# State loads in mid stage, packs from the diagonal down, and the MLP's normed input begun during the output projection

## The reference, cut to what matters

```python
def rmsnorm(x, g):
    y = xf * lax.rsqrt(jnp.mean(xf * xf, axis=-1, keepdims=True) + EPS)
    return y * g
...
for l in range(DEPTH):
    mix = mlstm_layer(...) if l < N_SELF else stick_breaking_attention(q, k_all, v_all, ...)
    h = h + mix @ w_out
    u = rmsnorm(h, norm_mlp[l]) @ w_up[l]
    h = h + jnp.square(jax.nn.relu(u)) @ w_down[l]
# stick-breaking, per head: A[t,s] = beta_ts * prod_{s<j<t}(1 - beta_tj), for s < t strictly
# mLSTM, per sequence: returns h and the final states (c, n, m)
```

## Time and profile before

| | us |
|---|---|
| median of 3 runs | 3212.4 |
| profiled execution, device time | 3211.99 |
| its span | 3210.2 |
| TensorE busy | 2914.1 (91%) |
| VectorE busy | 1363.2 (42%) |
| ScalarE busy | 857.8 (27%) |
| GpSimd busy | 769.2 (24%) |

### The profile page before, as it was taken

How to read it: one execution, slowest core, us unless ns; L and a number is a source line. 1 busy time by engine, 2 the same in 40 slices (tenths; PEclk the granted TensorE clock), 3 DMA queues, 4 the chain that set the end, 5 groups by cost and what they waited for, 6 DMA issues and landing times. The chain is left out here.

```text
span 3210.2 us, 49314 instructions
## 1 busy us (share of the span) xinstructions
PE 2914.1 (91%) x19749; PEld 2646.6 (82%) x19749; DVE 1363.2 (42%) x1993; ACT 857.8 (27%) x1677; POOL 769.2 (24%) x452
## 2 busy tenths in 40 slices
PE   5979698999999999988988889888799999999996
PEld 4968586989999999976666666666598999999995
DVE  4323233353334444344555554554525433334442
ACT  3111212131011111123545455545503111011114
POOL 3211120323322233331211121110032333322230
PEclk8999897999999999998999999999899999999997
DMA  5664413322222222223333333333411111111111
GB/s 154 189 153 138 87 34 15 107 88 84 91 91 91 91 91 91 91 76 100 110 100 105 106 106 109 97 108 86 148 57 40 47 46 40 45 46 46 46 46 60
DMA packets 362481, 277.66 MB, mean 86 GB/s; under 512 B 31394, under 2 KB 353954, under 8 KB 360290
## 3 DMA queue, kind: packets, MB, share of 16 engines
q1 hardware_dynamic: 341002, 258.18, 27.2%
q10 hardware_dynamic: 21336, 17.47, 2.6%
HBM read 251.58 MB, written 91.11 MB: 107 GB/s over the span
## 5 line engine op out<-in xcount | busy, mean ns | idle before, releaser
L162 POOL CAST w_hi<-w_raw 128x1024 fp32r<-128x1024 f32 x194 | 209.0, 1077 | 1725.7 <-PE bank L214 945.3
L212 PE MATMUL bank<-x_hi,w_hi 128*128 128x352 f32 x1872 | 605.2, 323 | 4.2 <-DVE p_q L1743 4.2
L214 PE MATMUL bank<-x_hi,w_lo 128*128 128x352 f32 x1872 | 602.0, 322 | 0.0
L213 PE MATMUL bank<-x_lo,w_hi 128*128 128x352 f32 x1872 | 601.5, 321 | 0.0
L212 PE MATMUL bank<-p_u_hi,w_hi 128*128 128x352 f32 x1536 | 496.5, 323 | 14.6 <-DVE p_u_lo L1947 14.6
L164 POOL TENSOR_TENSOR w_lo<-w_raw,w_hi 128x1024 fp32r<-128x1024 f32 x194 | 494.5, 2549 | 15.5
L213 PE MATMUL bank<-p_u_lo,w_hi 128*128 128x352 f32 x1536 | 495.5, 323 | 0.0
L214 PE MATMUL bank<-p_u_hi,w_lo 128*128 128x352 f32 x1536 | 495.3, 322 | 0.0
L1955 DVE TENSOR_TENSOR h<-bank,h 128x352 f32<-128x352 f32 x384 | 200.0, 524 | 492.4 <-PE bank L214 492.4
L1915 ACT ACTIVATE p_relu<-bank 128x352 f32<-128x352 f32 x192 | 89.3, 465 | 1042.7 <-PE bank L214 1032.9
L212 PEld LDWEIGHTS bank<-x_hi,w_hi 128*128 128x128 f32 x1872 | 352.0, 188 | 6.2 <-issue 6.0
(11 more groups left out here) (238 smaller groups left out, 4134.7 us busy)
## 6 DMA issues: line engine op xcount, KB each, us to landing
k_pages<-in_cache_k SPq DMA_DIRECT2D x64, 512.0 KB, 5.5
w_raw<-in_w_up SPq DMA_DIRECT2D x64, 512.0 KB, 4.0
v_pages<-in_cache_v SPq DMA_DIRECT2D x64, 512.0 KB, 4.6
w_raw<-in_w_down SPq DMA_DIRECT2D x64, 512.0 KB, 3.3
p_pages<-k_pages SPq DMA_DIRECT2D x256, 128.0 KB, 2.4
p_pages<-v_pages SPq DMA_DIRECT2D x256, 128.0 KB, 2.3
w_raw<-in_w_in_a SPq DMA_DIRECT2D x26, 512.0 KB, 4.2
h<-h_spill ACTq DMA_DIRECT2D x16, 528.0 KB, 6.5
```

The costliest lines, as they stand in the source:

```text
L162: pool.tensor_copy(m.whi[slot][:, :], m.wraw[slot][:, :]).then_inc(w.hi, 1)
L212: pe.matmul(bank[:, 0:TW], wh, xh, start=(k == 0), stop=False)
L213: pe.matmul(bank[:, 0:TW], wh, xl, start=False, stop=False)
L214: last = pe.matmul(bank[:, 0:TW], wl, xh, start=False, stop=(k == nk - 1))
```

## The change

State loads: the load of the next pair's state, with its two waits, stays at the stage's head for stage 0 alone; in stages 1 and 2 it stands behind ScalarE's copy of the `v` rows `(1, 2)`. Behind each stage's squares ScalarE preloads the table set with Ln and Exp.

Packs: their list is reversed (diagonal block first). A pack waits for the upper chunk's product if it is the first, and for the lower chunk's when it comes to block pair 1; start and stop of the accumulation follow the new order, and so does the wait for a free weights buffer.

Join: of the output projection's input, blocks 0 to 3 are split into `uhi`, `ulo` instead of `m.xhi`, `m.xlo`. ScalarE and VectorE make the MLP's `x_hi`, `x_lo` of block k < 4 right behind panel k's squares; block 4 follows behind the last tile, ahead of the last squares, and 5 to 7 behind them. The first MLP panel starts with k 0 to 3, and the sums of squares stand between k 3 and k 4.

```diff
-def dense_first(pe, m, w, n, slot, before, x):
+def dense_first(pe, m, w, n, slot, before, x, between=None):
...
     for k in range(KT):
+        if k == KT // 2 and between is not None:
+            between()
         pe.wait_ge(x, k + 1)
...
             for p in range(HP + 1):
-                if p + 1 < HP:
-                    act.wait_ge(state_in, 32 * (p + 1))
-                    if p:
-                        act.wait_ge(state_out, 64 * p)
-                    load_state(p + 1)
+                if p + 1 < HP and p == 0:
+                    act.wait_ge(state_in, 32)
+                    load_state(1)
...
                     if i == 1 and p:
                         inverse_rms(p - 1)
+                    if x == ("v", p, (1, 2)) and 0 < p < HP - 1:
+
+                        act.wait_ge(state_in, 32 * (p + 1))
+                        act.wait_ge(state_out, 64 * p)
+                        load_state(p + 1)
                 if p < HP:
                     squares(p)
+                    act.preload_act_table_set("natural_log_exp_and_others")
...
-    PACKS = [[(c, min(2, t + 1 - 2 * c)) for c in range(t // 2 + 1)] for t in TILE_AT]
+    PACKS = [[(c, min(2, t + 1 - 2 * c)) for c in range(t // 2, -1, -1)] for t in TILE_AT]
...
-                    n, c = e
-                    if c == 0:
-                        pe.wait_ge(a_ready, unit_no(p, n, len(CHUNKS[n]) - 1, 1) + 1)
+                    n, y = e
+                    c, blocks = PACKS[n][y]
+                    if y == 0 or c == 1:
+
+                        pe.wait_ge(a_ready, unit_no(p, n, 1 if len(CHUNKS[n]) > 1 and c < 2 else 0, 1) + 1)
...
-                                             start=(kb == 0), stop=(kb == tile), skip_group_check=True)
+                                             start=(x == 0 and i == 0), stop=(c == 0 and i == blocks - 1), skip_group_check=True)
...
-                        act.wait_ge(turned, TURN_NO["pack", pu, (nu, len(PACKS[nu]) - 1 if upper else min(1, len(PACKS[nu]) - 1))] + 1)
+                        act.wait_ge(turned, TURN_NO["pack", pu, (nu, len(PACKS[nu]) - (3 if upper else 1))] + 1)
...
+        HALF = KT // 2
+        yhi = [uhi[:, k, :] for k in range(HALF)] + [m.xhi[:, k, :] for k in range(HALF, KT)]
+        ylo = [ulo[:, k, :] for k in range(HALF)] + [m.xlo[:, k, :] for k in range(HALF, KT)]
...
-            norm_pe(pe, m, s)
-
-            dense_first(pe, m, w, KT, 0, USES_OUT, s.x)
+            dense_first(pe, m, w, KT, 0, USES_OUT, s.x, between=lambda: norm_pe(pe, m, s))
...
+            def x_high(k):
+                if k >= HALF:
+
+                    act.wait_ge(w.tile_ready, TILES_OUT)
+                act.activation(m.xhi[:, k, :], m.h[:, k, :], ACT.Copy, scale=gain[:, k:k + 1]).then_inc(s.hi, 1)
+
...
             for k in range(KT):
 
+                if k == KT - 1:
+                    x_high(HALF)
                 for t in range(NT):
                     act.wait_ge(w.tile_free[t], k + 1)
                 norm_square(act, m, s, m.h, k)
-
-            act.wait_ge(w.tile_ready, TILES_OUT)
-            norm_act_hi(act, m, s, m.h, gain)
+                if k < HALF:
+                    x_high(k)
+            for k in range(HALF + 1, KT):
+                x_high(k)
             norm_act_rs(act, m, s)
...
                     dve.tensor_tensor(ht, m.bank[t][:, 0:TW], ht, ALU.add).then_inc(w.tile_free[t], 1)
-                if k:
-                    norm_add(dve, m, s, k - 1)
-            norm_add(dve, m, s, KT - 1)
-
-            for t in range(NT):
-                dve.wait_ge(w.tile_free[t], USES_OUT)
-            norm_dve_lo(dve, m, s, m.h, gain)
+                if k == KT - 1:
+                    dve.wait_ge(w.tile_ready, TILES_OUT)
+                    x_low(HALF)
+                norm_add(dve, m, s, k)
+                if k < HALF:
+                    x_low(k)
+            for k in range(HALF + 1, KT):
+                x_low(k)
             dve.wait_ge(s.rs, 1)
```

48 lines of the change are left out of this document (36 added, 12 removed).

## The result

The changed kernel takes 3117.67 us (median of 4 runs, 3116.07 to 3122.69), beside 3211.53 for the kernel before on the same chip: a ratio of 0.9708 [0.9691, 0.9725]. The forecast was 3107, with a range of 3096 to 3127. The profiled execution has a span of 3114.5 us against 3210.2, so between these two executions the change brought 95.7 us of the 105.2 that the sum promised; between the medians it is 93.9.

What follows compares the result with a forecast made beforehand. TensorE, busy 91% of the span, was taken to bound the kernel, so only its idleness and half clock counted. 52.6 + 3.6 + 34.6 + 14.4 = 105.2 us off 3212.0 gave 3106.8, with 0.4 for the median 3107; range 3096 to 3127.

Steps and rivals of the forecast that it cites:

- The state loads: First mixer, stages 1 and 2: moving the loads removes waits of 23.6 + 24.2 us and the half clock, 52.6 us.
- four worries: First mixer: stores not landed, loads late, weight panel late (0 to 10 us a transition), head sums late (0 to 1).
- The preload: Fewer exposed table loads: stage 3 start 1.0, mixer's end 1.3, second mixer's first panel 1.3; sum 3.6 us.
- under 3 us in all: Sign of being right: the waits for decay weights at line 741 (743 after the change) fall below this total.
- The drain: Rival, 5%: each table switch also costs about 1.38 us, so removing three exposed switches brings 4 us more, 3103.
- The joins: Both joins of output projection and MLP: 5.0 us of idleness and 2.2 of half clock saved, 7.2 each, 14.4.
- The packs: Second mixer, slot 1: lower chunk's scores start 4.95 us earlier in each of seven pairs, 34.6 us.
- some 4 us at half clock, so 4.5 at full clock: Second mixer, slot 1: TensorE's 6.4 us from first pack to lower chunk's scores shrink to 4.5.
- whose copy other follow-ups cover: Second mixer: the last pack of even tiles becomes a full one, its copy covered by other follow-ups.
- The first rival: Second mixer, 12%: VectorE's and ScalarE's chain sets the following slots' pace, packs bring only 2 us a pair, 3127.
- The second mixer's start: First panel, waiting 4.18 us for the inverse norm: the preload removes an exposed table load, 1.3 us.

Runs made afterwards that it cites:

- the freed gates: Changed kernel, with ScalarE's upper-chunk gates in slots 1 to 3 freed from waiting for the lower chunk's product of the slot before; 3114.54 us.
- the kernel with one tile reversed: Changed kernel, with the order of chunks reversed for tile 7 alone and the other tiles in their old order; 3115.78 us.

## Why the prediction was right, and where it was off

**The state loads: right.** The term was 52.6 us, the stretch gave 52.5. The agreement to 0.1 us is luck, since the same stretch took 354.7 to 359.1 us in four profiles with the old code; some 50 is the size. Both halves of it are in the rows: the idleness (line 743 waits 3.8 us in all) and the half clock (1.00 in the windows behind the transition). Its four worries were each answered by a row: the stores had landed, the loads were early, the panel's split came at 236.54 and wasn't waited for, and the spread was not late.

**The preload: right in size, measured by its waits.** 2.5 us in stages 3 and 4, of 2.3, and 1.28 us at the second mixer's first panel, of 1.3. The reservation is that these 2 us are as large as what the clock does there by chance: 87.4, 87.3 and 89.0 us for the same stages in the changed kernel's two profiles and in the one with the freed gates, in code that is alike up to there, and 91.2 with the preload alone. What I expected to see at line 743, under 3 us in all, was a slip: of the 4.8 us at the start of stage 3 I had taken only 1.0 away, which leaves the 3.8 that is there. The drain that the Trainium skill (ScalarE: Activation LUTs, What ACT_TABLE_LOAD costs) puts on top of each switch did not show here either: 18 switches went from the final norm, which became 21.8 us shorter, and 18 x 1.283 is 23.1. With a drain of 1.38 us for each it would have been up to 48, more than the stage lasted.

**The joins: right, a little high.** 7.2 and 7.1 us, of 7.2 each. From wait to wait a join gave 7.0 and 7.1 us (52.5 in place of 59.5 and 59.6), and over all profiles the two stretches are 6.0 us shorter between the means. The wait was 0.82 in place of 0.65: the first matmul starts 0.26 us behind the addition's end (605.42 + 0.52 = 605.94).

**The packs: the step that failed.** The mechanism held link by link: the first pack waits 1.67 us, the new wait at line 1449 is 1.19, the scores of the lower chunk come 5.0 us earlier, and slot 1 gives 34.3 us. The term of 34.6 was a sum over slot 1 only. It took the half clock in the stall's wake as saved with the stall ("some 4 us at half clock, so 4.5 at full clock"; the trace has 5.1, up to 1615.2), put nothing for the slots behind, and multiplied by seven. In the runs a fall comes in slot 2 or 3 instead: six falls in six of seven pairs, where the kernel before had three falls in two pairs. These three falls more are 3.7 us (2.7 and 2.4 taken back in slots 2 and 3, less the 1.4 that follow). Over all profiles it is more: with the old order slots 2 and 3 had 5 falls in 28 pairs, and with all tiles reversed 25 in 28. In seven pairs the two slots together took 195.6 us against 203.1; that is 7.5 of the 12 us by which the term was too large, of which 1.4 are no falls: reversed packs in slot 2 cost 0.2 us in each pair, as the kernel with one tile reversed shows; the prediction had them covered ("whose copy other follow-ups cover"). A wait of 2.21 us for a value page in slot 5 of pair 1 makes most of the 2.3 us there; such a wait came in some profiles and not in others. And the mixer's end waits 1.87 us longer for VectorE. That this is the new order's isn't shown: with the old order the wait was 2.2 to 4.0 us in four profiles. The first rival falls: its 2 us a pair were 3.8 (26.4 by 7), and 3.6 between the means of all profiles. Pair 7's 3.8 us belong to none of this: in the three other kernels with the old order it also took 69.9 to 70.2 us, only the profile of before had 73.8, and the changed kernel's second profile had 73.2.

**The second mixer's start: an omission.** The prediction let 1.3 us go there, and it became 1.0 longer. TensorE waited 8.71 us for the squares instead of 5.86, and the reason stands on the time lines of VectorE, in the kernel before and then in the changed one, and of GpSimd in the changed one:

```profile
1439.03 6.13 DVE L293 TENSOR_TENSOR squares<-squares,square 128x1056 f32<-128x1056 f32 x3
...
1377.71 8.09 DVE L295 TENSOR_TENSOR squares<-squares,square 128x1056 f32<-128x1056 f32 x3
```

```profile
1381.45 3.23 POOL L164 TENSOR_TENSOR w_lo<-w_raw,w_hi 128x1024 fp32r<-128x1024 f32 x1
```

Three additions take 8.09 us where the same three took 6.13 before. With the freed gates, GpSimd's split came later against them, at 1386.80: the additions took 6.14, and a small operation behind them (line 1745) took 2.31 us in place of 0.16, as it had in the kernel before. There TensorE waited 6.2 us. It is the same collision with another victim, and the times of both engines say that GpSimd's start decides it. This stretch of code wasn't changed at all. The wait is 8.6 to 8.7 us in four profiles and 5.9 to 6.3 in eight. One of the eight is the kernel with one tile reversed, whose code is the changed kernel's up to there, so the same code has both. All four long waits come with the new join, though, so that it makes them likelier is open. The preload's 1.3 us behind that wait are there.

## What to carry to other kernels

Taking a stall of TensorE away need not keep its clock up. In the changed kernel's profile the clock stayed at 1.00 at the transitions of the first mixer and at the joins, where the stall had been; in the slots of the second mixer another fall came shortly behind. So keep the half clock as a possible cost until a profile shows the stretches behind the stall as well. Sum a term over the whole period of a loop and not over the slot with the stall: the neighbours took back 1.1 us of each 4.9. Profile more than one execution of the kernel before: its one profile made the gain of the packs look 6 us larger than the others do. And look through the whole list of table loads once a preload is known to hold: the largest further gain, 21.8 us, lay in a stage that the change didn't touch.

## What the runs showed of the hardware that was not expected

- **VectorE beside GpSimd.** An operation of VectorE with several inputs from SBUF (the on-chip memory that holds all tiles but TensorE's banks) that begins 0.02 us after GpSimd's took 3.50 us instead of 1.25 and ended behind it. That is the rule of the Trainium skill (SBUF — State Buffer, Who interferes with whom), by which the two share a pair of ports under an exclusive lock and a VectorE instruction with two SBUF inputs contends with a GpSimd instruction that reads SBUF. The trace agrees: 2.42 us of GpSimd's plus about 1.2 is 3.6. A 16-column `tensor_scalar` operation with one input waited too (2.31 us in place of 0.16).
- **The same code at the kernel's start waits for its first norm between 7.8 and 11.1 us** in twelve profiles. With a wait of 7.8 the seven additions of squares took 12.68 us, with 11.1 they took 14.64, beside GpSimd's splits. Together with the falls of the clock this is a part of the spread of one kernel's executions (3206 to 3223 us for the kernel before in one comparison of nine); how large a part isn't shown.
- **A fall of the clock in slots 2 and 3 costs nearly the same each time.** It is 1.1 to 1.3 us, with a mean granted clock of 0.89 to 0.91 over the slot, in all 35 falls of the nine profiles without freed gates. Its place varies between executions of one program, while there is about one for a pair of heads. With freed gates some slots 2 had more, up to 2.3 us at 0.83.
